# A depthwise convolution's shifted copies: written by GpSimd inside SBUF instead of through a table in DRAM

## The reference

```python
def _conformer_conv(h, p):
    z = h @ p["w_pw1"] + p["b_pw1"]
    a, g = jnp.split(z, 2, axis=-1)
    u = a * jax.nn.sigmoid(g)
    u = lax.conv_general_dilated(          # depthwise: 31 taps along the tokens
        u, p["w_dw"][:, None, :], window_strides=(1,),
        padding=((CONF_KERNEL // 2, CONF_KERNEL // 2),),
        dimension_numbers=('NWC', 'WIO', 'NWC'),
        feature_group_count=u.shape[-1]) + p["b_dw"]
    u = jax.nn.silu(_layernorm(u, p["ln_g"], p["ln_b"]))
    return u @ p["w_pw2"] + p["b_pw2"]
```

## Time and profile before

| | us |
|---|---|
| median of 3 runs | 1473.19 |
| lowest and highest of them | 1471.92, 1476.12 |
| the profiled execution | 1473.13 |
| its span in the trace | 1470.8 |
| granted TensorE clock, mean | 0.998 |

### The profile page before, as it was taken

One profiled execution on the slowest core, in us unless ns is written; L12 is line 12 of the kernel. 1 busy time (PEld: TensorE's weight loads), 2 busy tenths in 40 slices (PEclk: granted clock), 3 DMA queues, 4 the chain that ended last, 5 costly groups with the idle time before them and its releaser, 6 DMA issues.

```text
span 1470.8 us, 20379 instructions
## 1 busy us (share of the span) xinstructions
PE 1435.0 (98%) x8408; PEld 1207.8 (82%) x8408; DVE 1145.2 (78%) x1077; ACT 956.5 (65%) x936; POOL 51.9 (4%) x51
## 2 busy tenths in 40 slices
PE   6999999999999999999999999999999999999997
PEld 4778899998968778888888888888888888888885
DVE  3565744445886699988878889878888887988997
ACT  2454643333475777777787777777777778777773
POOL 0210011000001100000000000000000000000010
PEclk9999999999999999999999999999999999999999
DMA  9867776756866499999989999989999998999993
GB/s 374 297 245 266 264 243 229 228 173 208 295 229 254 149 353 374 375 391 375 375 350 374 375 383 377 375 339 385 375 373 391 376 376 349 373 376 391 385 412 125
DMA packets 102930, 476.51 MB, mean 324 GB/s; under 512 B 8396, under 2 KB 39260, under 8 KB 53680
## 3 DMA queue, kind: packets, MB, share of 16 engines
q1 hardware_dynamic: 99696, 465.86, 83.5%
q0 software_dynamic: 2560, 8.54, 1.7%
q10 hardware_dynamic: 576, 0.73, 0.2%
HBM read 469.96 MB, written 5.14 MB: 323 GB/s over the span
## 4 chain that ended last, share of the span: by engine, by line
PE 90%; DVE 4%; ACT 2%; DMA 2%; issue 1%; POOL 0%; ACTq 0%; DVEq 0%; POOLq 0%
PE bank L1750 21%; PE bank L1748 21%; PE bank L1749 21%; PE bank L1754 6%; PE bank L1756 5%; PE bank L1755 5%; PE bank L2301 2%; PE bank L1791 2%; DMA raw<-w_in 1%; PE bank L2086 1%; PE bank L2087 1%; PE bank L2088 1%; PE bank L1808 1%; PE bank L2266 1%; DMA const<-table 1%
## 5 line engine op out<-in xcount | busy, mean ns | idle before, releaser
L1613 DVE TENSOR_TENSOR low<-raw,high 128x2048 fp32r<-128x2048 f32 x333 | 749.2, 2287 | 106.7 <-ACT high L901 105.8
L901 ACT ACTIVATE high<-raw 128x2048 fp32r<-128x2048 f32 x333 | 631.5, 1921 | 99.7 <-DMA raw<-moe 98.5
L1748 PE MATMUL bank<-high,hidH 128*128 128x512 f32 x896 | 349.5, 390 | 0.0
L1750 PE MATMUL bank<-high,hidL 128*128 128x512 f32 x896 | 349.1, 390 | 0.0
L1749 PE MATMUL bank<-low,hidH 128*128 128x512 f32 x896 | 348.6, 389 | 0.0
L1754 PE MATMUL bank<-hidH,high 128*128 128x256 f32 x736 | 211.5, 287 | 3.1 <-DVE hidL L1066 1.3
L1755 PE MATMUL bank<-hidL,high 128*128 128x256 f32 x736 | 208.1, 283 | 0.0
L1756 PE MATMUL bank<-hidH,low 128*128 128x256 f32 x736 | 208.1, 283 | 0.0
L1750 PEld LDWEIGHTS bank<-high,hidL 128*128 128x128 f32 x896 | 168.2, 188 | 35.0
L1748 PEld LDWEIGHTS bank<-high,hidH 128*128 128x128 f32 x896 | 168.2, 188 | 34.7
L1749 PEld LDWEIGHTS bank<-low,hidH 128*128 128x128 f32 x896 | 168.2, 188 | 34.7
(11 more groups left out here) (250 smaller groups left out, 1221.7 us busy)
## 6 DMA issues: line engine op xcount, KB each, us to landing
raw<-moe SPq DMA_DIRECT2D x336, 1024.0 KB, 5.2
raw<-ada_w SPq DMA_DIRECT2D x40, 1024.0 KB, 5.8
raw<-ffn_gu SPq DMA_DIRECT2D x44, 512.0 KB, 5.1
raw<-ffn_down SPq DMA_DIRECT2D x11, 1024.0 KB, 5.1
raw<-ada_first SPq DMA_DIRECT2D x8, 1024.0 KB, 15.1
raw<-w_in SPq DMA_DIRECT2D x8, 1024.0 KB, 8.9
raw<-conv_pw SPq DMA_DIRECT2D x16, 512.0 KB, 4.8
raw<-w_o SPq DMA_DIRECT2D x4, 1024.0 KB, 6.9
```

The costliest lines, as they stand in the source:

```text
L901: a.activation(high[:, m % SPLITS, :], raw[:, n % RAWS, :], ACT.Copy).then_inc(S("high_ready"), 1)
L1613: v.tensor_tensor(low[:, n % RAWS, :], raw[:, n % RAWS, :], high[:, m % SPLITS, :].bitcast(F32), ALU.subtract).then_inc(S("low_ready"), 1)
L1748: pe.matmul(out, xh, wh, start=start, stop=False)
L1750: return pe.matmul(out, xl, wh, start=False, stop=stop)
```

## The change

The table in DRAM, its write, the wait for it and its four reads are taken out. In their place GpSimd waits for tile 2 and writes its 16 copies, and then waits for tile 3 and writes its 16, each copy one instruction from one quarter of the partitions of `uP` to another of `shifted`. TensorE's wait is now for each tile by itself: 16 copies before `conv_tile(2)`, 32 before `conv_tile(3)`.

```diff
-        conv_d = nc.dram_tensor("conv_rows", (2 * GROUPS, CG, TILES * UROW), F32).ap()
@@
-            i0, i1 = conv_tiles(1)
-            pool.wait_ge(S("glu_ready"), 2 * UC)
-            pool.dma_start(conv_d.rearrange("(k g) c x -> (g c) k x", g=GROUPS),
-                           uP[:, i0:i1].rearrange("p k t n -> p k (t n)")).then_inc(S("conv_kept"), 16)
-            pool.wait_ge(S("conv_kept"), 16)
-            for a in range(SHIFTS):
-                pool.dma_start(
-                    shifted[CG * a:CG * (a + 1), GROUPS * i0:GROUPS * i1].rearrange("c q t n -> c q (t n)")[:, :, 0:SHIFTED],
-                    conv_d.rearrange("q c x -> c q x")[:, :, a:a + SHIFTED]
-                ).then_inc(S("shifted_in"), 16)
+            for k in (2, 3):
+                i = ON_PE.index(k)
+                pool.wait_ge(S("glu_ready"), k + 1)
+                for a in range(SHIFTS):
+                    for g in range(GROUPS):
+                        st.mark(pool.tensor_copy(
+                            shifted[CG * a:CG * (a + 1), GROUPS * i + g].rearrange("c t n -> c (t n)")[:, 0:SHIFTED],
+                            uP[CG * g:CG * (g + 1), i].rearrange("c t n -> c (t n)")[:, a:a + SHIFTED]),
+                            "shifted_in")
@@ def conv_tile(k):
                 if u == 1:
-                    pe.wait_ge(S("shifted_in"), 16 * SHIFTS)
+                    pe.wait_ge(S("shifted_in"), SHIFTS * GROUPS * (i + 1))
```

## The result

The changed kernel takes 1479.45 us (median of 6 runs, 1477.6 to 1480.57) against 1473.41 us for the kernel before in the same comparison; the ratio is 1.0038, 95% interval 1.0028 to 1.0049. It is slower by 6.0 us, and 1479.2 was forecast. The sum was nearly right. How the 6 us come about was only half right, and that half is what the experiments are about.

What follows compares the result with a forecast made beforehand. TensorE, busy 98%, was taken to bound the kernel, with DVE's taps ending the stage. 29 collisions of 0.30 us, 8.7 us, less waits of 1.44 and 1.18, added 6.1 to 1473.13: 1479.2 us, range 1472.5 to 1487.0.

Steps and rivals of the forecast that it cites:

- The table off the path, its removal worth 0: DRAM table's copies of tiles 2 and 3 land some 6 us before TensorE needs them; removal costed at 0.
- Collisions of tap and copy, one to one: GpSimd copies and DVE taps with two SBUF operands exclude each other and alternate, one tap and one copy in 0.70 us.
- The copy: One GpSimd copy of 316 elements takes 0.49 us, bounds 0.36 to 0.75; 32 alone take 15.7 us, ending at 413.5.
- The price of one collision: Each copy costs DVE 0.30 us among the taps, 0.17 to 0.56 with the copy's bounds.
- the first rival: No collisions that count: a copy excludes DVE only while streaming, 0.1 us or less each; +0.3, 1473.4 us, chance 0.24.
- the main case: Taps and copies alternate, 0.30 us a copy taken; 0.17 to 0.40 us a copy gives +2.3 to +9, chance 0.50.
- 29 collisions, 8.7 us of DVE time: 29 of the 32 copies collide in DVE's taps and low part, at 0.30 us each; glu(2) comes 5.1 us late.
- What reaches the last tap: DVE's 8.7 us less its two waits, 1.44 for gate 3 and 1.18 for a high part, leave 6.1 us.
- TensorE follows ACT, at most 4.3 us late, and so is ready before DVE: From conv_tile(4) on TensorE follows ACT, ready for ln_sums by 444.0, before DVE at 447.0.
- Late next is DVE: At ln_sums, DVE's last tap ends the stage, 6.1 us late, and nothing behind gives it back.
- The wait of 4 to 5 us for a tap before `ln_sums`: Sign expected in the profile: TensorE waits 4 to 5 us there instead of 1.22.
- Starvation: DVE keeps SBUF access through its taps, GpSimd's copies come late, tile 3 ready at about 453: 1503 us, chance 0.04.

Runs made afterwards that it cites:

- experiment 1: Changed kernel with GpSimd's 32 copies replaced by 32 memsets of the same outputs, nothing read: 1473.22 us, ratio 0.9997 to the kernel before.
- Experiments 1 and 2: The second: changed kernel, copies kept, taps of tiles 0 and 1 accumulating in PSUM: 1473.33 us, ratio 0.9992 to the kernel before. The first is experiment 1.
- experiment 9: Changed kernel with each of the 32 copies cut from 316 to 158 elements: 1473.91 us in a single run, beside 1474.23 for the kernel before.
- experiment 5: Changed kernel with TensorE's sum of the ada rows moved one place down, behind conv_tile(4): 1476.99 us, ratio 1.0019 to the kernel before.
- experiment 4: Changed kernel with 16 spare products on TensorE before its wait for DVE's copy of the ada rows: 1476.53 us, ratio 1.0015 to the kernel before.
- experiment 10: Changed kernel with ACT's read-out of convolution tile 7 moved ahead of the second pw2 piece's high part: 1479.58 us, ratio 1.0036 to the kernel before.

## Why the prediction was right, point by point

- **The table off the path, its removal worth 0:** right, shown by experiment 1.
- **Collisions of tap and copy, one to one:** right, and the step that decides. Experiments 1 and 2 take away the one reader and the other, and each brings the time back to that of the kernel before. The Trainium skill, "SBUF — State Buffer", section "Who interferes with whom", describes it: two SBUF inputs on DVE contend with a GpSimd instruction that reads SBUF, not with one that only writes; the runs agree on both, 9.28 us with copies and 6.42 with memsets. The same section has the loser block fully, as the prediction says; for short instructions the runs differ, as the next points show, and the measurement decides.
- **The copy:** 0.49 us was taken, 0.44 measured, within the bounds; 32 of them alone would have been through in time.
- **The price of one collision:** mis-sized, 0.30 us taken, 0.19 measured (0.587 - 0.40). The sum put one instruction's remainder behind the other's reported end. The trace fits better with the fixed parts running beside the other engine's reading: 0.587 is then the tap's reading (256 elements, 0.27), the copy's (316 at 0.84 ns, 0.26) and 0.06 for two handovers. Only the copy's part was varied (experiment 9); the tap's 0.27 is an estimate at the rate of the low part, 2048 elements in 2.14 us, as in the prediction. This is the mechanism of the first rival, a copy that excludes DVE only while it streams. Its price of 0.1 us or less was too low, as the main case's 0.30 was too high.
- **29 collisions, 8.7 us of DVE time:** the count held, the time was 5.7 us (2.86 + 0.25 + 2.56). `glu(2)` came 3.1 us late (409.41 - 406.60, and 0.29 of offset) instead of 5.1.
- **What reaches the last tap:** 8.7 - 2.62 = 6.1 was forecast. Measured, the last tap ends 2.9 us later, 3.2 with the offset. The subtraction of the two waits was right in kind (1.44 gone whole, 0.95 of 1.18).
- **"TensorE follows ACT, at most 4.3 us late, and so is ready before DVE":** this step failed. TensorE does not only follow ACT there. It needs DVE's copy of the `ada` rows, which came 4.1 us late (3.8 in the rows, 0.29 of offset) with 0.15 us to spare. It stood for 3.97 us, lost 2.6 more to the clock, freed its ring slot late, and `ln_sums` ended 6.4 us late.
- **"Late next is DVE":** wrong in the changed kernel. The wait of 4 to 5 us for a tap before `ln_sums` is not there; TensorE goes into `ln_sums` late itself and then waits 0.7 us for ACT. It is true in experiment 5, where the sum was moved out of the way.

So two errors of about 3 us met. By its own steps with the right price, the prediction would have read 5.7 - 2.62 = 3.1 and 1473.1 + 3.1 = 1476.2 us, 3 us too low. That the change makes the kernel slower, and why DVE is late, was foreseen; that the sum came out within 0.3 us was luck. Of the stage's 6.4 us: 3.7 stay when the clock is kept up (experiment 4), 2.7 are the clock, and 0.7 of all of it passes through ACT's read-out (experiment 10). What the later stages added in the one profiled execution (8.0 us of span against 6.4) was not traced further; the medians differ by 6.0.

## What to carry to other kernels

An engine that is idle is not free if its instructions read SBUF beside DVE instructions with two SBUF operands: here 0.19 us of DVE for each copy of 316 elements and 0.06 for one of 158, and with one operand in PSUM nothing. When an engine will be late, go through every instruction on its queue and ask who waits for each, not only for the last; here the one that hurt was a side job between the taps. And price a wait of TensorE with what its clock does behind it.

## What was not expected of the hardware

- **The clock behind a short wait.** TensorE stood for 3.97 us; the granted clock fell to 0.50 while it stood and was back at 1.00 from 436 us on. The same eight products took 2.08 us against 1.16. Behind the 2.06 us in experiment 5 it showed 0.61, but behind the 1.83 us in the same run 1.00, and so behind the 1.22 us of the kernel before:

```profile
441.00:444.00 3.00, 3.00 (x14) 2.66 (x15) 2.29 (x1) 0.86 (x2) 0.00 (x0) 1.00 0.98 382
```

- **Alternation is fair and exact.** With both queues full, neither engine got two turns in a row: 0.587 us for each pair in both runs of taps, and a GpSimd copy that met a low part stood for it once (2.39 us). Starvation, a rival with 0.04, did not occur.
- **Not the whole instruction excludes.** The two long cases in the earlier trace rows looked as if it did. Short ones overlap in part: a tap and a copy take 0.48 and 0.44 us alone and 0.587, not 0.92, together.
